# First modulation computed in four chunks of two slices instead of two halves of four

## The reference, cut to what matters

```
ada = silu(c) @ w_ada + b_ada                     (once for the context vector, once for the latent one)
sh1, sc1, g1, sh2, sc2, g2 = split(ada, 6)
n   = rmsnorm(h, norm1_g) * (1 + sc1) + sh1
z   = n @ w_in                                     (17 chunks of 512 columns; v, i, q, k, ... are cut from it)
```

## Time and profile before

| what | us |
|---|---|
| median of three runs | 1107.72 |
| lowest and highest of them | 1102.82, 1109.83 |
| span of the profiled execution | 1102.2 |
| first matmul starts (from the span's start) | 13.41 |
| first matmul of v starts | 25.38 |
| first matmul of ic starts | 55.03 |

### The profile page before, as it was taken

One profiled execution on the slowest core, in us unless ns is written; L12 is line 12 of the kernel. 1 busy time (PEld: TensorE's weight loads), 2 busy tenths in 40 slices (PEclk: granted clock), 3 DMA queues, 4 the chain that ended last, 5 costly groups with the idle time before them and its releaser, 6 DMA issues.

```text
span 1102.2 us, 15099 instructions
## 1 busy us (share of the span) xinstructions
PE 1045.3 (95%) x4876; PEld 700.7 (64%) x4876; DVE 531.3 (48%) x1110; ACT 357.0 (32%) x481; POOL 151.8 (14%) x136
## 2 busy tenths in 40 slices
PE   4999999999899999999989999999999999999975
PEld 2489888788788898874645455454555555454532
DVE  2233544354698966944634334334344333333357
ACT  3333544326444535501423222222223222212101
POOL 0020232000000000000010322322323212111000
PEclk9999999999999999999999999999999999999998
DMA  9999777346555332740287999999999999999592
GB/s 354 394 292 358 114 115 108 136 177 207 205 182 186 114 124 96 235 166 1 95 360 271 374 403 400 414 412 401 414 416 417 411 400 418 413 408 387 234 408 107
DMA packets 88530, 306.62 MB, mean 278 GB/s; under 512 B 13399, under 2 KB 17751, under 8 KB 66465
## 3 DMA queue, kind: packets, MB, share of 16 engines
q1 hardware_dynamic: 68896, 270.63, 62.4%
q0 software_dynamic: 12256, 26.80, 10.5%
q10 hardware_dynamic: 7328, 8.55, 2.3%
HBM read 285.31 MB, written 36.85 MB: 292 GB/s over the span
## 4 chain that ended last, share of the span: by engine, by line
PE 61%; DVE 2%; issue 1%; ACT 1%; DVEq 0%
PE PS L2069 17%; PE PS L2071 8%; PE PS L2094 4%; PE PS L1958 4%; PE PS L2055 3%; PE PS L1705 3%; PE PS L2084 3%; PE PS L2086 2%; PE PS L2085 2%; PE PS L2026 2%; PE PS L2143 1%; PE PS L2110 1%; PE PS L1946 1%; PE PS L1947 1%; PE PS L1948 1%
## 5 line engine op out<-in xcount | busy, mean ns | idle before, releaser
L1105 POOL DMA_INDIRECT y_parts<-bigB,IDX x38 | 70.3, 1851 | 335.6 <-DVE bigB L1642 326.5
L2069 PE MATMUL PS<-bigB 128*128 128x512 f32 x224 | 101.7, 597 | 0.0
L1759 PE MATMUL PS<-bigB_r 128*128 128x384 f32 x288 | 98.6, 342 | 1.3 <-ACT bigB L791 1.3
L2071 PE MATMUL PS<-bigA,bigB 128*64 128x512 f32 x208 | 94.7, 598 | 3.7 <-issue 3.7
L1761 PE MATMUL PS<-bigB_r,bigA_r 128*128 128x384 f32 x288 | 96.5, 335 | 0.0
L1760 PE MATMUL PS<-nT_r,bigB_r 128*128 128x384 f32 x288 | 96.3, 334 | 0.0
L2072 PE MATMUL PS<-bigB 128*64 128x512 f32 x208 | 94.8, 598 | 0.0
L1642 DVE TENSOR_SCALAR bigB<-PS,bigD 128x1024 f32<-128x1024 f32 x40 | 51.3, 1284 | 89.8 <-PE PS L2086 55.1
L2069 PE MATMUL PS<-bigA,bigB 128*128 128x512 f32 x208 | 94.6, 597 | 0.0
L1250 DVE TENSOR_TENSOR bigA_r<-bigA,bigB_r 128x2048 fp32r<-128x2048 f32 x18 | 41.3, 2292 | 97.6 <-ACT bigB_r L817 97.6
L1608 DVE TENSOR_TENSOR bigB<-bigB,PS 128x256 f32<-128x256 f32 x40 | 16.8, 421 | 134.8 <-ACT bigB L1001 134.8
(11 more groups left out here) (370 smaller groups left out, 2116.4 us busy)
## 6 DMA issues: line engine op xcount, KB each, us to landing
bigA<-in_w_in SPq DMA_DIRECT2D x17, 2048.0 KB, 10.4
bigB<-in_w_gate SPq DMA_DIRECT2D x27, 1024.0 KB, 11.1
bigB<-in_w_up SPq DMA_DIRECT2D x27, 1024.0 KB, 19.2
bigB<-in_w_down SPq DMA_DIRECT2D x27, 1024.0 KB, 19.4
bigA<-in_w_gate SPq DMA_DIRECT2D x26, 1024.0 KB, 7.5
bigA<-in_w_up SPq DMA_DIRECT2D x26, 1024.0 KB, 16.3
bigA<-in_w_down SPq DMA_DIRECT2D x26, 1024.0 KB, 19.2
bigA<-in_w_ada SPq DMA_DIRECT2D x8, 2048.0 KB, 10.1
```

Of the source, the lines that this page charges most:

```text
L1105: pool.indirect_dma_start(y_parts, bass.IndirectOffsetOnAxis(ap=IDX[:, p, 1:2], axis=0), YS[:, p % 2, :], None, bounds_check=T * TOPK - 1, ...
L1759: mm(out, wh, nh, start=(k == 0), stop=False)
L2069: last = mm(PS[:, 2 + b, :], XT[:, b, k, :], GU_W[s][:, :, k, :], start=first, stop=stop)
L2071: mm(PS[0:HALF, 2 + b, :], XT[:, b, k, 0:HALF], GU_W[2][:, :, k, :], start=first, stop=stop)
```

## The change

```diff
 def schedule():
-    s = [("csilu",), ("norm1",), ("unit", 0), ("xt", 0), ("modt", 0), ("unit", 1), ("xt", 1), ("modt", 1), ("mods", 0)]
-    for k in range(KD):
-        s.append(("vk", k))
-        if k in (1, 2):
-            s.append(("unit", k + 1))
-        if k == 3:
-            s += [("modt", 2), ("modt", 3), ("mods", 1), ("ic_split",), ("n_high",)]
+    s = [("csilu",), ("norm1",)]
+    for c in range(EARLY):
+        s.append(("unit", c))
+        if c == 0:
+            s.append(("xt", 0))
+        s += [("modt", c), ("mods", c)]
+        if c == 0:
+            s.append(("xt", 1))
+        if c == EARLY - 1:
+            s += [("ic_split",), ("n_high",)]
+        s += [("vk", 2 * c), ("vk", 2 * c + 1)]
...
-                    for c in (2 * n, 2 * n + 1):
+                    for c in (0,) if n == 0 else (1, 2, 3):
...
-                for k in range(k0, k0 + 4):
+                for k in range(k0, k0 + 2):
...
-                if k0 > 0:
+                if k0 + 2 == KD:
...
-                    hf = ev[1]
+                    c = ev[1]
...
-                    dve.wait_ge(modt_ready, hf + 1)
-                    mod_columns(0, slice(4 * hf, 4 * hf + 4), cc(C_N1), hf + 1,
+                    dve.wait_ge(modt_ready, c + 1)
+                    mod_columns(0, slice(2 * c, 2 * c + 2), cc(C_N1), c + 1,
...
-                    modulate(4 * hf)
+                    modulate(2 * c)
...
-                    for k in range(4 * hf, 4 * hf + 4):
-                        at = c * WCH + k % 4 * P
-                        last = mm(PS[:, 7, (s_ * KD + k) * 2:(s_ * KD + k) * 2 + 2], ADA[:, at:at + P], pair, start=True, stop=True)
-                    if s_ == 1:
-                        last.then_inc(modt_ready, 1)
+                    for s_ in range(2):
+                        for k in (2 * c, 2 * c + 1):
+                            at = c * WCH + (2 * s_ + k % 2) * P
+                            last = mm(PS[:, 7, (s_ * KD + k) * 2:(s_ * KD + k) * 2 + 2], ADA[:, at:at + P], pair, start=True, stop=True)
+                    last.then_inc(modt_ready, 1)
...
-    first = w_ada[:, 0:2 * D].reshape(D, 2, P, 2, 4).transpose(0, 3, 1, 4, 2).reshape(D, 2 * D)
+    first = w_ada[:, 0:2 * D].reshape(D, 2, P, EARLY, 2).transpose(0, 3, 1, 4, 2).reshape(D, 2 * D)
```

More of the change, by code:

```diff
@@ L954, in _ @@
                     m = ev[1]
-                    act.wait_ge(mod_ready, 3)
+                    act.wait_ge(mod_ready, EARLY + 1)
                     act.wait_ge(n2_ready, m)
@@ L1470, in _ @@
                     link(nc.vector.tensor_tensor(MODP[:, :, 0, :], MODP[:, :, 0, :], MODP[:, :, 1, :], ALU.add))
-                    mod_columns(2, slice(0, KD), cc(C_N2), 3, MODP[:, :, 0, :].rearrange("p s (v k) -> p s v k", v=2))
+                    mod_columns(2, slice(0, KD), cc(C_N2), EARLY + 1, MODP[:, :, 0, :].rearrange("p s (v k) -> p s v k", v=2))
                 elif st == "wout":
@@ L1791, in _ @@
                     c = ev[1]
-                    hf, s_ = c // 2, c % 2
                     pe.wait_ge(unit_taken, c + 1)
                     pe.wait_ge(in_x, 32)
-                    for k in range(4 * hf, 4 * hf + 4):
-                        at = c * WCH + k % 4 * P
-                        last = mm(PS[:, 7, (s_ * KD + k) * 2:(s_ * KD + k) * 2 + 2], ADA[:, at:at + P], pair, start=True, stop=True)
-                    if s_ == 1:
-                        last.then_inc(modt_ready, 1)
+                    for s_ in range(2):
[3 more added lines that the diff above has]
+                    last.then_inc(modt_ready, 1)
                 elif st == "vk":
```

## The result

The changed kernel took 1118.96 us (median of 6 runs, 1111.22 to 1120.07) beside 1109.69 for the kernel before (6 runs): ratio 1.0088, 95% interval 1.0062 to 1.0113. It is 9.3 us slower by the medians (1118.96 against 1109.69); the forecast was 1116.1, 8.4 above a median before of 1107.7, in a range of 1107 to 1122. A second measurement of the same kernel (e8) gave less, 1.0044. The profiled execution has a span of 1109.4 us, 7.2 above the one of before. That run took 1111.22 us; the other five took 1116.84 to 1120.07.

What follows compares the result with a forecast made beforehand. The prediction took the order of instructions on TensorE, not data, to bound the stretch from 25 to 55 us. Exposed chains 3.9 plus clock 4.5 gave 8.4 us slower: 1107.7 + 8.4 = 1116.1 us, range 1107 to 1122.

Steps and rivals of the forecast that it cites:

- The start up to v: Start of the kernel: v's first matmul comes at 21.8 us instead of 25.38, a gain of 3.6 us.
- The pairs, and what is new behind each: v on TensorE: two vk 5.32 us plus an exposed chain 5.46, so 10.78 per chunk; 3.9 us slower without the clock.
- Halving the mods' columns: VectorE's modulation work per chunk: no gain taken, bounds none or 0.3 us each.
- The clock: TensorE behind the three new pauses: all followed by half clock, 4.5 us more, bounds 0 to 4.8.
- The term for one pause: Half clock behind each new TensorE pause in v: 1.5 us each, bounds 0 and 1.6.
- ic's split: ScalarE and VectorE at v's end: ic's weight split arrives with the ic units; cost 0, bounds 0 and 1 us.
- The clock does not fall: Rival for v's pauses: three exposed chains but no or one slowdown, 3.9 to 5.5 us slower, 1112 to 1113; chance 0.25.
- It does what it says: Rival for v: pauses somehow filled, v begins and ends 3.6 us earlier, 1104 us; chance 0.03.
- Faster through the clock: Rival: no new pause paid, two later slowdowns missed, 0.3 us saved per chunk; -0.7 us, 1107.0; chance 0.04.

Runs made afterwards that it cites:

- e8: The changed kernel, unchanged, run again for a second profile: 1113.40 us, ratio 1.0044 to the kernel before.
- e4: The changed kernel with the swap of loads undone, v weights again issued third behind ada chunks 0 and 1: 1122.18 us, ratio 1.0112 to the kernel before.
- e1: The changed kernel plus nine unread matmuls of 384 columns in the pauses behind units 1 to 3: 1111.45 us, ratio 1.0022 to the kernel before.
- e7: The kernel before, unchanged, run again for a second profile: ratio 0.9999.
- e2: The changed kernel with each next chunk's ada unit moved between the two vk of a chunk, hiding only its copy: 1108.17 us, ratio 1.0004 to the kernel before.
- e3: The changed kernel with units and modts moved ahead of earlier vk on TensorE, so no pause is left: 1102.68 us, ratio 0.9951 to the kernel before.

## Why the prediction was right

*The start up to v.* Right: v at 21.73, forecast 21.8. The swap of loads costs nothing here and is needed for that start: without it v begins 2.4 us later (e4).

*The pairs, and what is new behind each.* Right: a chunk at full clock takes 10.65 to 10.67 us from vk to vk (21.73 to 32.38), forecast 10.78; the pause is 0.72 + 1.05 + 1.63 = 3.40 us, forecast 3.5. Halving the mods' columns saved 0.01 us. e1 shows the sum alone, v's end at 59.68 against 59.53, and the runs' full parts put the changed kernel 4.6 and 4.9 us above the one before. The forecast's figure for this is 3.9 + 1.6 = 5.5, since its 55.60 held one slowdown.

*The clock.* That pauses are paid again through the clock is right and is shown by e1, where matmuls in the pauses took the slow pairs away while the chains stayed as long. The size for all three together was close in the first profile (4.5 forecast, 1.7 + 3.0 = 4.7) and too small in the second (1.5 + 1.7 + 2.9 = 6.1, with ic at 65.74, outside the forecast's 59 to 64). The term for one pause was mis-sized: bounds of 0 to 1.6 us, where the last one cost 3.0 and 2.9. The forecast's reason for expecting all three to be paid, that they are as long as the pause that was paid, did not hold: of equal pauses the first went unpaid in the first profile, the pause of before with its 1.64 us wait went unpaid in e7, and a shorter one of 2.6 us was paid in e2. What the forecast also missed is that the kernel before pays varying amounts: its profile had one slowdown in this stretch, e7's none, and its 26 runs spread over 11 us with the clock.

A single profile is one draw of this, and 8.4 landing near 9.3 is in part luck: the second measurement gave 0.44%, about 5 us. Set beside the splits, the forecast is 5.5 us full and 4.5 - 1.6 = 2.9 us more clock than before; measured were 4.6 and 4.2 the first time, 4.9 and 1.3 the second. The forecast time of 1116.1 lies 2.9 below the measured 1118.96, and 2.0 of this is that the kernel before itself came out at 1109.69 and not at 1107.7.

The Trainium skill's rule from "TensorE: Matmul & The Clock Gate", section "HAM oscillation — how this bites in real kernels", that a kernel of bursts and waits pays the transition at each round, is what these traces show at the three pauses of e8 and at two of three in the first profile. At the first pause of the first profile, at two of three in e2 and at both in e7 nothing was paid, so here the rule does not hold at every round; the page's rounds wait for transfers, these for ScalarE and VectorE with small matmuls between.

*ic's split.* Cost 0 was right with the slowdowns, as ic started 0.56 us ahead of the end of the last pair; at full clock it is 0.6 us (e1) and 0.3 us (e2), inside the bounds of 0 to 1.

*The rivals.* "The clock does not fall" gave 3.9 to 5.5 and is what e1 builds by force: 1.8 us above the kernel before by the medians, 5.6 us more full and 3.3 us less clock. The full part is the rival's figure. Of the 3.3 us, the one slowdown that the earlier trace rows shows in this stretch is worth 1.7 (12.26 against e7's 10.57); where the rest comes from is not shown. "It does what it says", v earlier by 3.6 at its end, needs pauses that are filled; e3 fills them and ends v 4.3 us earlier than in the profile of before, 2.6 without the slowdown of that profile; the full part falls by 2.3. "Faster through the clock" was not seen in any run of the changed kernel, the fastest of which took 1111.22 us. Its sum takes off 1.2 us for four chunks of 0.3, where only three pauses are exposed: 0.9.

## What to carry to other kernels

Cutting a dependent step in finer chunks starts the consumer earlier, but each chunk brings its own chain of producer, copy, small matmul and vector work, and where an engine works through its list in order, as TensorE does in this kernel, that chain is exposed unless other work is placed between its links. Cut finer only together with an order in which the next chunk's producer runs ahead of this chunk's consumer; then the same cut was worth 4 to 7 us here instead of a loss of 5 to 9. Where TensorE must pause for a few microseconds again and again, allow for half clock in the matmuls behind each pause, as something that may or may not come (here 0 to 3 us a pause). Profile each kernel more than once, and compare kernels by span times granted clock beside the plain times.

## What was not expected of the hardware

Nine matmuls that compute nothing useful made the kernel faster, 1111.2 us against 1116.2 on the mean of all runs of each, by keeping the granted clock at 1.00 through pauses of 3.4 us. The same pause, to 0.01 us, was followed by the half clock in one execution and not in the next: in the kernel before 12.26 and 10.57 us for the same 24 records behind a wait of 1.64 us. And one pause can cost about 3 us: TensorE stayed at 0.50 in every full microsecond from 55 to 61 although it was busy without a break from 55.41 on, and the last pair took 8.39 us where 5.42 is the full-clock time.
